# Two score banks side by side and one exponential over both maps of a key block

## The reference

```python
h = rms_norm(x, g_pre)
proj = h @ w_in                                   # (S, 5648), split into q, k, v, gates of both branches
# branch A: differential attention, 4 heads, two maps m = 0, 1 of width 64, causal, ALiBi
s = einsum('bhmqd,bhmkd->bhmqk', qi, k) * scale   # scores of both maps
s = where(dist >= 0, s - slopes * dist, -inf)
p = softmax(s)
oa = einsum('bhqk,bhkd->bhqd', p[:, :, 0] - lam * p[:, :, 1], v)
ya = (rms_norm(oa, g_sub_a) * (1 - lam_init) * silu(za)) @ w_up_a
# branch B: gated linear attention in chunks, 4 heads
yb = (rms_norm(ob, g_sub_b) * silu(zb)) @ w_up_b
y = sigmoid(gate_a) * ya + sigmoid(gate_b) * yb
return x + rms_norm(y @ w_out, g_post)
```

## Time and profile before

| | |
|---|---|
| device time, 3 runs | median 1646.62 us (lowest 1643.45) |
| the profiled execution | 1651.65 us, span of its slowest core (core 1) 1650.0 us |
| spans of the 8 cores in it | 1627.0 to 1650.0 us, mean granted TensorE clock 0.958 to 0.969 |
| PE busy | 1430.6 us, 87% of the span, 10576 matmuls |
| ACT busy | 852.6 us, 52%, 1714 instructions |
| DVE busy | 711.4 us, 43% |
| POOL busy | 465.3 us, 28% |
| DMA | 207 MB, mean 126 GB/s |

### The profile page before, as it was taken

How to read it: one execution, slowest core, us unless ns; L and a number is a source line. 1 busy time by engine, 2 the same in 40 slices (tenths; PEclk the granted TensorE clock), 3 DMA queues, 4 the chain that set the end, 5 groups by cost and what they waited for, 6 DMA issues and landing times.

```text
span 1650.0 us, 27769 instructions; the slowest of 8 cores (1627.0 to 1650.0 us)
## 1 busy us (share of the span) xinstructions
PE 1430.6 (87%) x10576; PEld 747.7 (45%) x10576; DVE 711.4 (43%) x1449; ACT 852.6 (52%) x1714; POOL 465.3 (28%) x469
## 2 busy tenths in 40 slices
PE   4868687899899997999879998799997999987888
PEld 2324333444445543555445554455543555543443
DVE  3546645653565343542435324353233441242434
ACT  4244343434453555355464665646666657666632
POOL 1024422253225221432204322043311240220342
PEclk9888889999999998999989999999999999999999
DMA  9966487423542335222442223422234312223113
GB/s 286 236 194 179 133 272 233 141 90 115 192 141 90 103 115 179 90 90 93 156 134 66 90 90 122 162 75 76 80 101 153 98 59 76 78 91 115 52 65 115
DMA packets 75437, 207.43 MB, mean 126 GB/s; under 512 B 7984, under 2 KB 26672, under 8 KB 75312
## 3 DMA queue, kind: packets, MB, share of 16 engines
q1 hardware_dynamic: 75312, 205.66, 38.9%
HBM read 173.12 MB, written 32.51 MB: 125 GB/s over the span
## 4 chain that ended last, share of the span: by engine, by line
PE 60%; DVE 12%; ACT 10%; DMA 9%; issue 3%; POOL 3%; SPq 2%; DVEq 0%; POOLq 0%; ACTq 0%
PE ps_q L270 30%; PE ps_f L270 18%; PE ps_oa L270 12%; DMA out<-sb_scr 4%; ACT sb_PT L964 4%; DMA sb_KT<-w_in 3%; DVE sb_scr L841 2%; SPq L364 1%; ACT sb_junk L859 1%; ACT sb_ztmp L613 1%; DVE sb_scr L861 1%; DVE sb_wring L377 1%; DVE sb_rz L990 1%; DMA sb_KT<-w_out 1%; DVE sb_tmpo L992 1%
## 5 line engine op out<-in xcount | busy, mean ns | idle before, releaser
L964 ACT ACTIVATE sb_PT<-ps_q 128x512 bf16<-128x512 f32 (+3 forms) x685 | 363.0, 568 | 254.8 <-PE ps_q L270 170.7
L270 PE MATMUL ps_oa<-sb_V,sb_PT 128*128 128x129 bf16 x4224 | 345.8, 222 | 15.1 <-ACT sb_PT L964 7.5
L270 PEld LDWEIGHTS ps_oa<-sb_V,sb_PT 128*128 128x128 bf16 x4224 | 287.1, 99 | 143.4 <-issue 35.2
L964 ACT ACTIVATE sb_PT<-ps_f 128x512 bf16<-128x512 f32 (+3 forms) x467 | 255.6, 564 | 150.5 <-PE ps_q L270 75.1
L270 PE MATMUL ps_q<-sb_hT,sb_wring 128*128 128x512 bf16 x1040 | 267.3, 391 | 26.0 <-ACT sb_wring L373 8.6
L270 PE MATMUL ps_q<-sb_QT,sb_KT 64*128 64x512 bf16 (+3 forms) x685 | 163.7, 368 | 45.1 <-ACT sb_scr L636 20.5
L270 PE MATMUL ps_f<-sb_hT,sb_wring 128*128 128x512 bf16 x752 | 189.3, 386 | 5.9 <-ACT sb_hT L591 3.7
L809 POOL TENSOR_TENSOR sb_yT<-sb_scr 128x512 bf16<-128x512 f32 x64 | 81.2, 1270 | 397.1 <-DVE sb_scr L807 397.1
L270 PE MATMUL ps_q<-sb_wring,sb_hT 128*128 128x512 bf16 x616 | 166.6, 407 | 21.4 <-DVE sb_szA L614 12.3
L270 PEld LDWEIGHTS ps_q<-sb_hT,sb_wring 128*128 128x128 bf16 x1040 | 94.8, 100 | 141.2 <-issue 62.5
L270 PE MATMUL ps_f<-sb_QT,sb_KT 64*128 64x512 bf16 (+3 forms) x467 | 134.5, 364 | 16.4 <-DVE sb_yT L614 3.1
(11 more groups left out here) (171 smaller groups left out, 1859.3 us busy)
## 6 DMA issues: line engine op xcount, KB each, us to landing
sb_wring<-wsc SPq DMA_DIRECT2D x204, 512.0 KB, 3.6
sb_xb<-x SPq DMA_DIRECT2D x60, 512.0 KB, 4.5
sb_KT<-w_in SPq DMA_DIRECT2D x88, 256.0 KB, 7.7
out<-sb_scr SPq DMA_DIRECT2D x32, 512.0 KB, 3.3
wsc<-sb_wring SPq DMA_DIRECT2D x30, 512.0 KB, 6.0
sb_KT<-w_out SPq DMA_DIRECT2D x16, 256.0 KB, 6.2
sb_KT<-w_up_a SPq DMA_DIRECT2D x8, 256.0 KB, 7.6
sb_KT<-w_up_b SPq DMA_DIRECT2D x8, 256.0 KB, 8.0
```

What stands on the lines that cost most here:

```text
L270: P.op("pe", lambda e: e.matmul(out=out_, lhsT=lhsT, rhs=rhs, start=start, stop=stop, **kw), reads=reads, writes=writes)
L964: act(lambda e, pp=pp, m=m, c0=c0, b=b, cbias=cbias: e.activation(out=PT[pp][:, m, c0:512], in_=BANK[b][:, c0:512], func=AF.Exp, bias=cbia ...
```

## The change

The five shared banks become two tensors of two neighbouring banks each (`psQ[0]` = q0, q1; `psQ[1]` = q2, q3) and one single bank `f`. The scores of the two maps of a key block go to the two halves of one pair, and one activation reads both halves (128 x 2 x 512) and writes both halves of `PT`. So `emit_qk` no longer takes whichever banks are idle: it needs both pairs idle. Before it, a new loop hands out filling units until no q bank is held by a half-finished chain. `bank_take` now prefers `f` for filling work, if `f` is idle and at least one other bank was taken since its last turn; else it takes the first of the idle list.

```diff
-        psQ = [PSM(f"q{i}", [128, 512], F32) for i in range(3)]
-        psF = [PSM(f"f{i}", [128, 512], F32) for i in range(2)]
+        psQ = [PSM(f"q{i}", [128, 1024], F32) for i in range(2)]
+        psF = PSM("f", [128, 512], F32)
...
-        idle_banks = ["f0", "f1", "q0", "q1", "q2"]
+        idle_banks = ["f", "q0", "q1", "q2", "q3"]
+        turn = {"n": 0, "f": -9, "q0": -9, "q1": -9, "q2": -9, "q3": -9}
 
         def bank_take():
-            return idle_banks.pop(0)
+            b = idle_banks[0]
+            if "f" in idle_banks and turn["n"] - turn["f"] >= 2:
+                b = "f"
+            idle_banks.remove(b)
+            turn["n"] += 1
+            turn[b] = turn["n"]
+            return b
...
+        def pair_free(i):
+            return f"q{2 * i}" in idle_banks and f"q{2 * i + 1}" in idle_banks
+
+        def pair_order():
+            age = [max(idle_banks.index(f"q{2 * i}"), idle_banks.index(f"q{2 * i + 1}")) for i in range(2)]
+            return [0, 1] if age[0] < age[1] else [1, 0]
...
             todo = []
+            order = pair_order()
             for kb in kbs:
...
+                pr = order[kb % 2]
                 for m in range(2):
-                    b = bank_take()
+                    b = f"q{2 * pr + m}"
+                    idle_banks.remove(b)
...
-                act(lambda e, pp=pp, m=m, c0=c0, b=b, cbias=cbias: e.activation(
-                    out=PT[pp][:, m, c0:512], in_=BANK[b][:, c0:512], func=AF.Exp, bias=cbias, scale=1.0), [b], [f"PT{pp}_{m}"])
-                bank_give(b)
+                act(lambda e, pp=pp, c0=c0, pr=pr, cbias=cbias: e.activation(
+                    out=PT[pp][:, :, c0:512], in_=psQ[pr][:, :].rearrange("p (m c) -> p m c", m=2)[:, :, c0:512], func=AF.Exp,
+                    bias=cbias, scale=1.0), [f"q{2 * pr}", f"q{2 * pr + 1}"], [f"PT{pp}_0", f"PT{pp}_1"])
+                bank_give(f"q{2 * pr}")
+                bank_give(f"q{2 * pr + 1}")
...
+            def step():
+                c, f, _ = units.pop(0)
+                f()
+                done[0] += c
+                if c > 0:
+                    run_post()
...
                     if prev:
                         emit_pv(*prev[1])
+                    while not (pair_free(0) and pair_free(1)):
+                        step()
                     emit_qk(t, h, (kb, kb + 1))
```

More of the change, by code:

```diff
@@ L250, in _build @@
         block = es.enter_context(nc.Block())
-        BANK = {"q0": psQ[0], "q1": psQ[1], "q2": psQ[2], "f0": psF[0], "f1": psF[1], "a0": poa[0], "a1": poa[1], "a2": poa[2]}
-        idle_banks = ["f0", "f1", "q0", "q1", "q2"]
+        BANK = {"q0": psQ[0][:, 0:512], "q1": psQ[0][:, 512:1024], "q2": psQ[1][:, 0:512], "q3": psQ[1][:, 512:1024], "f": psF[:, :],
+                "a0": poa[0][:, :], "a1": poa[1][:, :], "a2": poa[2][:, :]}
+        idle_banks = ["f", "q0", "q1", "q2", "q3"]
+        turn = {"n": 0, "f": -9, "q0": -9, "q1": -9, "q2": -9, "q3": -9}
         def bank_take():
-            return idle_banks.pop(0)
+            b = idle_banks[0]
[5 more added lines that the diff above has]
+            return b
         def bank_give(b):
             idle_banks.append(b)
+        def pair_free(i):
[3 more added lines that the diff above has]
+            return [0, 1] if age[0] < age[1] else [1, 0]
         def falloc():
@@ L960, in emit_qk @@
                     mm(BANK[b][:, c0:c0 + 128], ident[:, :], negm[:, :], False, True, ["ident", "negm"], [b], skip_group_check=True)
-            for kb, r, c0, m, b in todo:
+            for kb in kbs:
+                r = kb - 4 * t
+                c0 = 0 if r < 0 else 128 * r
+                pr = order[kb % 2]
                 pp = kb % 2
                 cbias = SLOPES[h] * (128.0 * r - 129.0)
-                act(lambda e, pp=pp, m=m, c0=c0, b=b, cbias=cbias: e.activation(
-                    out=PT[pp][:, m, c0:512], in_=BANK[b][:, c0:512], func=AF.Exp, bias=cbias, scale=1.0), [b], [f"PT{pp}_{m}"])
-                bank_give(b)
+                act(lambda e, pp=pp, c0=c0, pr=pr, cbias=cbias: e.activation(
[3 more added lines that the diff above has]
+                bank_give(f"q{2 * pr + 1}")
         def emit_pv(t, h, kb):
```

## The result

The changed kernel takes 1772 to 1777 us (its profiled execution 1773.42 us, the forecast was 1767); the ratio to the kernel before is 1.0765, 95% interval 1.0701 to 1.0828.

What follows compares the result with a forecast made beforehand. The prediction took PE, in its strict order, as the bound. Its terms, 123 - 24 + 40 - 15 - 5 + 1 = 120 us, on 1651.65 gave 1772, and with the median 5 us lower 1767 us, range 1690 to 1820.

Steps and rivals of the forecast that it cites:

- The bound and the size of the gain: PE bounds the kernel; wider exponentials save ACT 46 us, worth -5 us of kernel time, ends 0 and -46.
- Scores behind an eviction: Scores needing all four q banks wait on PE for evictions of just-filled banks: 132 us against 9 before, +123 us.
- Filling behind filling: Filling chains waiting for a bank an earlier filling chain used: 64 us before, 40 after, -24 us.
- Values and filling behind an exponential: Values and filling chains on PE wait longer for the pair's wide exponential: +40 us, ends 0 and 79.
- Cover and clock: Scores' waits in the first 276 us fall beside DMA, -15 us; lower PE clock after waits, +1 us, ends 0 and 80.
- the relief of 5: Wider exponentials shorten the time where PE waits for ACT: -5 us.
- Rival 4: Waits before and behind scores also lower PE's clock, mean under 0.94: +80 us, 1847 us; chance 0.13.
- the signs that the forecast named: In the changed profile: ACT busy some 40 us less, PE idle up 100 us or more, scores waiting for evictions.
- Rivals 2 and 3: New PE waits replace old ones, 1659 us, chance 0.08; ACT's relief wins, 1601 us, chance 0.03.

Runs made afterwards that it cites:

- e1: Changed kernel with the two maps' exponentials separate again, each releasing its own bank; median 1750.6 us, ratio to before 1.0620.
- e2: Kernel before plus the new loop alone, run ahead of the scores until all five banks are idle; median 1710.5 us, ratio 1.0374.
- e4: Kernel before with scores issued one key block at a time, same five banks and separate exponentials; 1610.6 to 1612.6 us, ratio 0.9780.
- e6: Changed kernel with silu's DVE half reading ztmp twice, freeing the bank after ACT alone (wrong silu result); median 1763.4 us, ratio to before 1.0682.
- e7: Changed kernel with both key blocks' values together before the scores, loop ahead of them, filling behind the scores; median 1705.8 us, ratio to before 1.0341.
- e8: Kernel before with both key blocks' values together right before the scores and all filling behind the scores; 1617.8 and 1624.1 us, ratio 0.9823.
- e10: Kernel before with silu's DVE half reading ztmp twice, freeing the bank after ACT alone (wrong silu result); 1641.4 us profiled, ratio 0.9921.
- e5: Kernel before with scores leaving the oldest bank to filling when all five are idle, taking the last filled one; median 1690.7 us, ratio 1.0251.

## Why the prediction was right

**The bound and the size of the gain** held: PE stayed the bound, and ACT's 32 us brought nothing (the forecast had given 5, and 46 as the most).

**Scores behind an eviction, +123.** I set each PE instruction of both traces beside the program's order and added up the distances of starts beyond what the matmuls take among themselves: a value 56 ns, a filling matmul of 512 columns 216, a pair of scores 222 (its second matmul starts 3 ns behind its first), and 95 more where scores follow another kind. Scores that reuse a filled bank cost 78 us before and 182 after: +104. The direction and the place are as forecast, the composition is partly luck. The answer times price evictions that begin at once. Of the waits of a quarter microsecond or more, those behind evictions that began within 0.3 us of the chain's end went from 12 (8 us) to 119 (91 us): +83, where the forecast has +123. Some 17 us of this gap have a source in the forecast's own rows: it put 0.45 us for eight values between chain and scores, and rows 4 and 5 show 0.55, because the change to scores takes 0.1 more; in the changed kernel the same 0.1 stands between a filling matmul and scores. At 0.1 in each of 184 steps that is an estimate of 17 us of cover that the forecast left out. Against this, 43 waits (85 us) stand behind evictions that began late, before 38 (67 us): +17, which the forecast had only in its upper end. Here one from the changed kernel:

```profile
1374.29 1.03 PE L285 MATMUL ps_q<-sb_wring,sb_hT 128*128 128x512 bf16 x4
1374.99 0.60 ACT L628 ACTIVATE sb_ztmp<-ps_f 128x512 f32<-128x512 f32 x1
1375.25 0.39 PE L285 MATMUL ps_q<-sb_QT,sb_KT 64*128 64x512 bf16 x2
1375.62 0.69 DVE L629 SCALAR_TENSOR_TENSOR sb_yT<-sb_ztmp,ps_f 128x512 bf16<-128x512 f32 x1 [1.76 <-ACT sb_ztmp L628]
1376.40 0.60 ACT L628 ACTIVATE sb_ztmp<-ps_q 128x512 f32<-128x512 f32 x1 [0.81 <-DVE sb_yT L629]
1376.89 1.02 ACT L985 ACTIVATE sb_PT<-ps_q 128x1024 bf16<-128x1024 f32 x1
1377.03 0.69 DVE L629 SCALAR_TENSOR_TENSOR sb_yT<-sb_ztmp,ps_q 128x512 bf16<-128x512 f32 x1 [0.72 <-ACT sb_ztmp L628]
1377.86 0.39 PE L285 MATMUL ps_q<-sb_QT,sb_KT 64*128 64x512 bf16 x2 [2.22 <-DVE sb_yT L629]
```

The chain in the q bank stops issuing some 0.1 us before the scores of 1375.25, and its silu starts at 1376.40, since the one buffer `ztmp` is still read by the silu before; and the exponential of the first pair, ready long before, queues behind it on ACT.

**Filling behind filling, -24**: 111 us before, 90 after by the same sum, -21. The pattern of the earlier trace rows is still there in the changed kernel at 1488.20, with the same 0.51 us, now in bank f.

**Values and filling behind an exponential, +40**: values directly behind scores went from 3 to 21 us (27 steps, in most of which the first value starts 0.91 us after the last score; the forecast had 1.15), values behind filling from 14 to 27, filling in an exponential's bank from 44 to 56: +43. By e1 some 23 us of the loss hang on the exponential's width.

**Cover and clock, -15 and +1**: values behind values went from 23 to 14 us, which is all the cover that the sum shows, and other filling work cost 3 us more. The terms measured, 104 - 21 + 43 - 9 + 3, give 120 of the 122 us between the two profiled executions. So the scores' term was 19 us too high, the cover 6 us too large, and the relief of 5 has no row of its own; that the whole fits so well is luck, since these errors cancelled. Rival 4 did not come: the mean of the cores' clocks went from 0.963 to 0.954, far from its bound of 0.94.

Of the signs that the forecast named, two came out smaller: ACT's busy time fell by 32 us and not by 40, and PE's idle time by the page rose by 84 us and not by 100, as 38 us of the waits lie inside its busy time.

The Trainium skill (Perfetto Trace Analysis, Optimizing Scalar/DVE Operations) had both sides of this change: an access overhead of about 51 ns per ScalarE operation on PSUM, and that breaking instructions up may help where that engine is not saturated. The trace agrees with the first (32.3 us of ACT for 576 operations, 56 ns each) and e1 with the second (23 us less with the exponentials broken up).

**Rivals 2 and 3** fell with the result. Where single edits were priced by counting, the sign was always right and the size was off by 24 to 78%: too high in e2 (95 us counted, 60 measured), e4 (55, 38), e6 (26, 10), e7 (120, 68), e8 (45, 29) and e10 (17, 13), too low in e5 (23, 41). The forecast of the whole was better than its method.

## What to carry to other kernels

Before banks are tied into groups for a wider instruction, ask which work is then forced into the bank used last: a bank costs its eviction's answer (here 0.95 to 1.70 us, more where the evicting engine's queue stands), and the matmul engine pays whatever it has no other work for. Count, for each reuse in program order, how much work lies in between. On an engine that was not the bound, 32 us of saved work were worth nothing here, and taking banks in smaller groups (two at a time in place of four) gained 2.2% with no instruction changed.

## What was not expected of the hardware

Putting the same matmuls in more, shorter runs has a price. Within a run of values one starts 0.056 us after the other; the first score behind a value starts 0.152 us after it, in nearly every case and alike in before, the changed kernel, e1 and e4. Behind a filling matmul it is 0.311 in place of 0.216. In e4 there are 572 changes from values to scores in place of 287, at 0.1 us each, 27 us more in sum. That would cover the 17 us by which e4 missed its forecast, but it was not tested by itself.

Few waits hold much of PE's lost time: in the kernel before, 16 reuses of a bank that cost over 2.5 us each make 74 us, in the changed kernel 19 make 82. Several of them have one cause, the one shown for e7: ACT stands for a store of the output before it can evict a bank, for 7.93 and 7.77 us in the kernel before (at 1255.62 and 1496.57), 6.19 and 7.61 in the changed kernel (at 1102.71 and 1353.24), 9.23 and 6.76 in e4. No order of banks that was tried removes them.
